# Gates and branch products with the tokens stationary and 512 weight columns streaming

## The reference, cut to what matters

```python
for l in range(2):
    h = _rmsnorm(x, g_mix[l])                       # x: 256 tokens x 1024
    proj = h @ w_in[l]                              # 1024 x 6656
    gate_pre, a_in, na_qkv, dil_qkv, swa_q, swa_kv = split(proj)   # gate_pre: 256 x 4096
    y_a = conformer_conv(a_in)                      # 31 taps, layer norm, silu
    y_b, y_c, y_d = three attentions of 4 heads     # each 256 tokens x 256
    branch[n] = y_n @ w_branch[l][n]                # four products 256x256 @ 256x1024
    gates = sigmoid(gate_pre.reshape(256, 4, 1024) + gate_b[l])
    mixed = sum_n(gates[n] * branch[n])
    x = x + mixed @ w_out[l]
    ...                                             # then the feed-forward part
```

## Time and profile before

| | us |
|---|---|
| median of 3 runs (1650.99 to 1652.85) | 1652.69 |
| the profiled execution's own time | 1651.02 |
| its span, first to last instruction | 1649.3 |
| PE busy | 1604.1 (97%) |
| DVE busy | 1119.4 (68%) |
| ACT busy | 891.5 (54%) |
| POOL busy | 421.6 (26%) |

### The profile page before, as it was taken

How to read it: one execution, slowest core, us unless ns; L and a number is a source line. 1 busy time by engine, 2 the same in 40 slices (tenths; PEclk the granted TensorE clock), 3 DMA queues, 4 the chain that set the end, 5 groups by cost and what they waited for, 6 DMA issues and landing times. The chain is left out here.

```text
span 1649.3 us, 26655 instructions
## 1 busy us (share of the span) xinstructions
PE 1604.1 (97%) x10765; PEld 1440.8 (87%) x10765; DVE 1119.4 (68%) x1587; ACT 891.5 (54%) x1410; POOL 421.6 (26%) x457
## 2 busy tenths in 40 slices
PE   8999999999999999999999999999999999999999
PEld 7868899987877889998888888999888888999997
DVE  6876665645576665655578978777646897867763
ACT  7565544434365455443456756666445684656652
POOL 3401100002341120000146902244204691214430
PEclk9999999999999999999999999999999999999999
DMA  9423366566330236665555345666446444466652
GB/s 352 154 77 129 102 204 185 178 202 206 108 127 27 77 103 179 186 189 188 177 193 166 129 153 161 182 185 191 179 153 219 164 135 149 141 202 190 186 179 76
DMA packets 287386, 267.38 MB, mean 162 GB/s; under 512 B 12320, under 2 KB 247584, under 8 KB 287008
## 3 DMA queue, kind: packets, MB, share of 16 engines
q1 hardware_dynamic: 287264, 265.69, 50.2%
HBM read 264.61 MB, written 1.05 MB: 161 GB/s over the span
## 5 line engine op out<-in xcount | busy, mean ns | idle before, releaser
L146 DVE TENSOR_TENSOR w_lo<-w_raw,w_hi 128x2048 fp32r<-128x2048 f32 x243 | 566.7, 2334 | 263.6 <-ACT w_hi L145 258.7
L145 ACT ACTIVATE w_hi<-w_raw 128x2048 fp32r<-128x2048 f32 x243 | 460.9, 1901 | 227.1 <-PE bank L538 125.5
L1999 PE MATMUL bank<-h_hi,w_hi 128*128 128x256 f32 x1984 | 565.6, 285 | 5.9 <-DVE mix_gates L2838 2.2
L2000 PE MATMUL bank<-h_lo,w_hi 128*128 128x256 f32 x1984 | 561.2, 283 | 0.0
L2001 PE MATMUL bank<-h_hi,w_lo 128*128 128x256 f32 x1984 | 561.1, 283 | 0.0
L1999 PEld LDWEIGHTS bank<-h_hi,w_hi 128*128 128x128 f32 x1984 | 380.3, 192 | 13.6 <-issue 13.1
L2000 PEld LDWEIGHTS bank<-h_lo,w_hi 128*128 128x128 f32 x1984 | 380.5, 192 | 0.1
L2001 PEld LDWEIGHTS bank<-h_hi,w_lo 128*128 128x128 f32 x1984 | 380.5, 192 | 0.0
L465 PE MATMUL bank<-w_hi,h_hi 128*128 128x512 f32 (+1 forms) x288 | 113.0, 392 | 3.8 <-DVE w_lo L242 2.1
L2645 POOL TENSOR_TENSOR mix_conv<-mix_conv,mix_gates 128x512 f32<-128x512 f32 x60 | 109.2, 1821 | 23.8 <-ACT mix_gates L2682 15.8
L3058 POOL TENSOR_TENSOR cffn_hidden<-cffn_conv 128x256 f32<-128x256 f32 x44 | 73.6, 1674 | 155.7 <-ACT cffn_conv L3089 155.7
(11 more groups left out here) (442 smaller groups left out, 2804.6 us busy)
## 6 DMA issues: line engine op xcount, KB each, us to landing
w_raw<-in_w_in SPq DMA_DIRECT2D x48, 1024.0 KB, 4.9
w_raw<-in_ffn_w_in SPq DMA_DIRECT2D x88, 512.0 KB, 4.7
w_raw<-in_w_up SPq DMA_DIRECT2D x88, 512.0 KB, 4.8
w_raw<-in_ffn_w_out SPq DMA_DIRECT2D x22, 1024.0 KB, 4.9
w_raw<-in_w_down SPq DMA_DIRECT2D x22, 1024.0 KB, 4.9
w_raw<-in_nsa_w_in SPq DMA_DIRECT2D x10, 1024.0 KB, 5.3
w_raw<-in_mem_w_kv SPq DMA_DIRECT2D x8, 1024.0 KB, 5.0
w_raw<-in_w_branch SPq DMA_DIRECT2D x8, 1024.0 KB, 4.7
```

Of the source, the lines that this page charges most:

```text
L145: return act.activation(hi, raw, ACT.Copy)
L146: return dve.tensor_tensor(self.lo[:, cut_slot, 0:k * n], raw, hi.bitcast(F32), ALU.subtract)
L1999: pe.matmul(out, h, hi[:, f, :], start=(f == 0), stop=False)
L2000: pe.matmul(out, h, lo[:, f, :], start=False, stop=False)
```

## The change

- **Gates.** A gate job is now a chunk of 4 x 128 rows by 512 gate columns. The tokens are stationary, in two groups of 128 (t), and the 512 columns stream: 2 x 4 x 3 = 24 matmuls, with two jobs for one set q of 512 columns. The result has tokens on the partitions. DVE takes the two banks of a set in a pair, behind the odd job: times the token's factor plus a bias row, `scalar_tensor_tensor`. Bias rows are loaded by 8 more DMAs, spread over the partitions, in three batches with waits on SP. Gate banks turn over 0, 2, 3.
- **Attention.** Values use bank 1 only, transposed pairs bank 6 only; layer norm has bank 7. The waits are one item closer, and DVE splits the values ahead of its copy.
- **Branch products.** Four groups of (half of the features, token group), four branches each, into four banks: tokens stationary, 512 weight columns streaming. DVE multiplies each by its gates, POOL adds the four (3 additions of 128 x 512 a group), PE transposes the sum back (4 transposes a group), ACT rounds it, DVE subtracts. ACT opens the gates of a group in one instruction of 128 x 2048.
- **Output projection.** It waits for the subtraction of group 2 ahead of its first row, makes the last group's transposes ahead of its third row, and waits for that group's subtraction ahead of its fifth.

```diff
     def value(self, m):
-        return self.k.bank[m % 2][:, 0:S]
+        return self.k.bank[1][:, 0:S]
...
-        if m >= 2:
-            pe.wait_ge(self.y_lo, m - 1)
+        if m:
+            pe.wait_ge(self.y_lo, m)
...
-                if j >= 2:
-                    pe.wait_ge(self.copied, j - 1)
+                if j:
+                    pe.wait_ge(self.copied, j)
...
             between(dve, i)
+            if i >= 5 and i % 2:
+                self.dve_values(dve, (i - 5) // 2)
             if 1 <= i <= n:
                 self.dve_copy(dve, i - 1)
-            if i >= 5 and i % 2:
-                self.dve_values(dve, (i - 5) // 2)
...
-        AHEAD, LN_STEP, OPEN = 2, 9, 2
-        gate_banks = [0, 1] + [2, 3] * 4 + [2] + [3] * 5
+        AHEAD, LN_STEP, LN_BANK = 2, 9, 7
+        GROUPS = [(half, t) for half in range(2) for t in range(T)]
+        BRANCHES = [(1, 2, 3, 0)] + [(0, 1, 2, 3)] * 3
+
+        def gate_bank(q, t):
+            return k.bank[(0, 2, 3)[(2 * q + t) % 3]]
...
+                def second_bias(sp):
+                    sp.wait_ge(turn.turned, 6)
+                    load_bias(sp, range(1, 5), gate_bias_in[1])
+
+                def third_bias(sp):
+                    sp.wait_ge(att.masked, 8)
+                    load_bias(sp, range(5, 8), gate_bias_in[2])
...
+                for n in range(len(GROUPS)):
+                    mixed = branch_product(n, 0)
+                    for place in range(1, 4):
+                        pool.wait_ge(mixed_m, 4 * n + place + 1)
+                        if place > 1:
+                            pool.wait_ge(mixed_p, 3 * n + place - 1)
+                        pool.tensor_tensor(mixed, mixed, branch_product(n, place), ALU.add).then_inc(mixed_p, 1)
...
-                    if j < len(gate_chunks):
-                        if j == 12:
+                    if j % 2 and j < len(gate_chunks):
+                        q = j // 2
...
+                        for t in range(T):
+                            dve.scalar_tensor_tensor(out=gates[:, t, q, :], in0=gate_bank(q, t)[:, :],
+                                                     scalar=rows.rstd[:, t:t + 1], in1=gate_bias[q], op0=ALU.mult,
+                                                     op1=ALU.add).then_inc(gated, 1)
...
+                for n in range(len(GROUPS)):
+                    for place in range(4):
+                        multiply(dve, n, place)
+                        if place == 1:
+                            if n >= 2:
+                                mixed_rest(dve, n - 2)
+                        if place == 2 and n < 3:
+                            w.cut_to(dve, (mix_chunks[2], mix_chunks[3], residual.first)[n])
+                mixed_rest(dve, 2)
+                w.cut_to(dve, residual.first + 1)
+                mixed_rest(dve, 3)
...
+                    for t in range(T):
...
+                        if part_of == 0 and 2 * q + t >= 3:
+                            pe.wait_ge(gated, 2 * q + t - 2)
+                        for row in range(4):
+                            f = 4 * part_of + row
+                            x_hi, x_lo = h_hi[:, f, t * P:(t + 1) * P], h_lo[:, f, t * P:(t + 1) * P]
+                            out = gate_bank(q, t)[:, :]
+                            pe.matmul(out, x_hi, whi[:, row, :], start=(f == 0), stop=False)
+                            pe.matmul(out, x_hi, wlo[:, row, :], start=False, stop=False)
+                            ins = pe.matmul(out, x_lo, whi[:, row, :], start=False, stop=(f == KD - 1))
...
+                def mixed_ready_for(pe, f):
+                    if f == 0:
+                        pe.wait_ge(mixed_lo, 3)
+                    if f == 2:
+                        mixed_turn(pe, 3)
+                    if f == 4:
+                        pe.wait_ge(mixed_lo, 4)
```

More of the change, by code:

```diff
@@ L943, in dve_copy @@
         dve.tensor_copy(free(self.k.turned[:, :, :], [[2 * S, 2], [S, T], [1, P]], j % 2 * P),
[L944 removed]
+                        free(self.k.bank[6][:, :], [[S, 2], [P, T], [1, P]])).then_inc(self.copied, 1)
     def dve_values(self, dve, m):
@@ L2697, in _, with open_gates, mixed_round @@
                 project.act(act, squares, hurry=3)
[L2699 to L2702, removed]
+                def open_gates(act, n):
+                    half, t = GROUPS[n]
+                    group = gates[:, t, 4 * half:4 * half + 4, :]
+                    act.activation(group, group, ACT.Sigmoid).then_inc(opened, 1)
+                def mixed_round(act, n):
+                    half, t = GROUPS[n]
+                    act.wait_ge(mixed_turned, n + 1)
+                    act.activation(h_hi[:, 4 * half:4 * half + 4, t * P:(t + 1) * P],
+                                   product_bank(n, 3)[:, :].rearrange("p (f q) -> p f q", q=P), ACT.Copy)\
+                       .then_inc(mixed_hi, 1)
                 w.round_to(act, gate_chunks[2])
@@ L2884, in _ @@
                    .then_inc(ln_lo, 1)
-                att.dve_values(dve, 5)
                 gate(dve, 15)
[L2888 to L2896, removed]
-                    else:
[L2898 to L2908, removed]
-                        dve.wait_ge(mixed_m, 2 * j + 2)
-                        dve.tensor_tensor(part[:, 1, 0:512], k.bank[3][:, :], part[:, 1, 0:512], ALU.add).then_inc(mixed_d, 1)
-                        dve.wait_ge(mixed_d, j)
-                        dve.tensor_tensor(part[:, 1, 0:S], part[:, 1, 0:S], part[:, 1, S:2 * S], ALU.add).then_inc(mixed_d, 1)
-                    if j >= 3 and j % 2 == 1:
-                        w.cut_to(dve, mix_chunks[0] + j // 2 + 2)
-                    if j:
-                        mixed_rest(j - 1)
@@ new lines, in _ @@
+                for n, (half, t) in enumerate(GROUPS):
+                    chunks = mix_chunks[2 * half:2 * half + 2]
+                    if n >= 2:
+                        pe.wait_ge(mixed_m, 4 * (n - 2) + 4)
+                    for place, branch in enumerate(BRANCHES[n]):
+                        if n == 0 and place == 0:
+                            pe.wait_ge(att.y_lo, 6)
+                        if n == 0 and place == 3:
+                            pe.wait_ge(ln_lo, 2)
+                        if n == 1 and place == 0:
+                            pe.wait_ge(gated, 16)
+                        if n >= 2 and place == 3:
+                            pe.wait_ge(mixed_lo, n - 1)
+                        if t == 0:
+                            w.wait_cut(pe, chunks[branch // 2])
+                        whi, wlo = w.halves(chunks[branch // 2])
+                        out = product_bank(n, place)[:, :]
+                        for row in range(2):
+                            f, r = 2 * branch + row, (2 * branch + row) % 4
+                            y, l = y_hi[:, f, t * P:(t + 1) * P], y_lo[:, f, t * P:(t + 1) * P]
+                            pe.matmul(out, y, whi[:, r, :], start=(row == 0), stop=False)
+                            pe.matmul(out, y, wlo[:, r, :], start=False, stop=False)
+                            ins = pe.matmul(out, l, whi[:, r, :], start=False, stop=(row == 1))
+                        if t == 1 and branch % 2 == 1:
+                            ins.then_inc(w.used, 1)
+                        else:
+                            ins.then_inc(mixed_ready, 1)
+                        if n and place == 2:
+                            mixed_turn(pe, n - 1)
```

150 lines of the change are left out of this document (80 added, 70 removed).

## The result

| | before | after |
|---|---|---|
| median of 4 runs, taken in turn (us) | 1652.77 | 1670.26 |
| lowest to highest | 1650.99 to 1654.34 | 1669.58 to 1671.16 |
| profiled execution (span) | 1651.02 (1649.3) | 1671.16 (1669.4) |

The changed kernel takes 1.0107 times as long, 95% interval 1.0089 to 1.0124. Another set of runs of it gave 1670.66 and the same 1.0107 (1.009 to 1.0124). I had forecast 1663.0, at most 1669: the direction is right, the time lies above the range. In what follows a layer is timed from its own first gate job, which starts at 868.76 and 1286.69 before, at 872.20 and 1298.10 after.

What follows compares the result with a forecast made beforehand. PE, busy 97%, was taken as the bound, with DVE setting the pace up to step 5. Per layer +4.85 to the branch products and +1.1 after made +5.95, +11.9 on 1651.02, so 1663; range 1649 to 1669.

Steps and rivals of the forecast that it cites:

- Pitch of the wide form: Gate matmuls of 512 columns start every 0.2267 us, so each of 16 gate jobs saves 0.32.
- Gates on DVE: 16 scalar-times-plus-bias operations at 0.68 us each replace 16 multiplications, now in pairs in even steps.
- wait before gate job 12: PE's 1.11 us wait for the bank that layer norm used goes, as layer norm has bank 7.
- The mid-job wait: In steps 2 and 4 PE waits inside a gate job for DVE's pair, using up its lead; no extra cost.
- V(1): PE's values in step 5 wait about 3 us for DVE's value subtraction and start 5.4 later (3.8 to 6.2).
- the lag of the masks: DVE's masks of step 5, begun at 926.30 before, come 1.6 us later (0 to 2.4).
- From V(1) to the branch products: PE sets the pace: nine gate jobs -2.9, layer norm's bank wait -1.1, value waits in odd steps +3.45.
- Branch products: Wide matmuls -1.3, added transposes +1.7, old waits -1.2, late end 1.9: sum +1.1 us a layer (-0.5 to +2.5).
- The wait at the first row: The output projection waits for DVE's subtraction of group 2, taken as 1.9 us (1.6, or 2.3 if slowed).
- rival 1: Value waits fall into gaps or DVE's lag shrinks, PE's work remains: -7.0 a layer, 1637 or 1642 us; chance 0.13.
- 2 (it cancels): DVE catches up sooner and half of the odd waits is hidden: +0 to +1.5 a layer, 1651 to 1655; chance 0.10.
- Rival 3: GpSimd's additions bound the mixing, at 2.0 us each with DVE's splits at 3.1: +3 a layer, 1669; chance 0.12.

Runs made afterwards that it cites:

- experiment 3: The changed kernel with the gates turning over four banks up to set 3, bank 7 added: 1670.92 us, ratio 1.011.
- experiment 10: The changed kernel with unread matmuls filling PE's waits ahead of the values in steps 5, 7, 9, 11 and in gate job 4: 1665.86 us, ratio 1.0077.
- experiment 5: The changed kernel with group 2's sum turned into bank 0, so the output projection needn't wait for that group's subtraction: 1667.52 us, ratio 1.009.
- experiment 2: The kernel before with all values in bank 1, the wait one item closer and DVE's split ahead of its copy: 1680.56 us, ratio 1.0169.
- experiment 8: The changed kernel once more, unaltered: 1670.66 us.
- experiment 7: The changed kernel with values split a step earlier, group 2's sum turned into bank 0, four gate banks up to set 3: 1649.25 us, ratio 0.9979.
- experiment 1: The changed kernel with the values of m=1 in bank 7, so two value waits reach two steps back again: 1659.2 us, ratio 1.0035.
- experiment 4: The changed kernel with unread matmuls in two waits, 9 in gate job 4 and 14 ahead of V(1): 1668.14 us, ratio 1.0093.
- experiment 9: The kernel before with all values in one bank and their split a step earlier, at the end of the even step: 1652.74 us, ratio 0.9998.

## Why the prediction was wrong

- **Pitch of the wide form**: right, 0.227. A job between attention pieces takes 5.66 instead of 5.91 to 5.95, so 0.25 to 0.29 and not 0.32 each.
- **Gates on DVE**: right in the price, 1.41 a pair, and there is no wait before gate job 12. The mid-job wait was foreseen, as PE's lead being used up, and experiment 3 shows that it is.
- **V(1)**: right in place and cause, and near in size, in part by luck. Less the 3.44 by which layer 0 began later, the masks stand at 927.65 (said 927.9), V(1) at 928.9 (said 929.1): +5.1, in layer 1 +5.8, for +5.4. I said 3 us of wait; it is 3.25. But the lag of the masks has other parts than I said. In layer 0 nothing of it had come up by the masks of step 4 (51.15 us behind the first gate job, 51.23 before), where I had +0.9. All of the 1.35 comes in step 4: 0.7 from the pair, as said, 0.7 from the division (1.73 instead of 1.02) and 0.4 from the weight split (3.35 instead of 2.93), both of which I had left as they were, less idle time of 0.35.
- **From V(1) to the branch products** is the step that failed: the sum had -2.9 - 1.1 + 3.45 = -0.55, measured +1.4 in both layers. In layer 0 the odd steps with a value wait are 3.75 longer for 3.45, steps 10 and 12 are 1.6 shorter for 1.1, and the nine jobs, but for the clock, 2.35 shorter for 2.9: together 0.35 off. The term that isn't in the sum is PE's clock: gate job 7 took 7.12 for 5.66, V(1) 1.13 for 1.02, 1.6 together. I priced a wait at its length. I noted the clock at the higher level in every slice and didn't ask what idle stretches of 3 us, which the kernel before doesn't have in these layers, would do to it.
- **The clock in the kernel before.** I took the page's slices of 41 us at their word. The kernel before has stretches at the lower level itself, outside the mixing layers. From 417.2 to 420.6 it follows an idle time of 1.42 and falls among matmuls of 75 columns. From 461.5 to 468.4 PE had been making matmuls of 32 columns since 459.49, and behind them wide ones start every 0.427 us. Windows of 2 us show it; columns as above:

```profile
462.00:464.00 2.00, 2.00 (x11) 0.50 0.75 242
...
466.00:468.00 2.00, 2.00 (x6) 0.50 0.00 0
```

- **Branch products**: +1.1 up to the output projection, +1.45 up to its last transposes, for +1.1 said. The wait at the first row is 1.47 for 1.9; the products start every 0.227 us as said, but the 96 take 22.45 instead of 21.8, because 0.3 are waited for GpSimd's first sum and the first starts behind each turn are further apart.
- **Start of the sum.** I added to the profiled 1651.0, though the median is 1652.7. This alone put the forecast 1.7 us low, as the prediction states.

Together: the sum gave 1663. Of what it missed, 1.7 come from where it started and 4.4 to 4.8 from the clock (experiment 10 against the changed kernel); and the filled kernel is 13.1 above the kernel before, where the sum had 11.9, so 1.2 are from the other terms. The range's top, 1669, and the sum of all high ends, 1673, took in longer waits but nothing behind them.

**The rivals.** 1 (streaming wins) and 2 (it cancels) fell with the order of DVE: the masks of step 5 come 1.35 later and not at 926. With the order mended the change gives 1651.7 and, with 3 and 5, 1649.2, not the 1637 of rival 1, since up to V(1) PE runs at DVE's pace and what its gates save there is spent waiting: up to V(1) the last one takes 56.3 for 55.0, from V(1) to the branch products 65.5 for 68.1, and 1.6 of the 65.5 are the clock.

Rival 3 (GpSimd the bound of the mixing) came close. The additions, lines of POOL from 1001 to 1023, changed kernel, and its first group in the timeline:

```profile
L2687 POOL TENSOR_TENSOR mix_feat<-mix_feat 128x512 f32<-128x512 f32 x6 | 13.4, 2235 | 28.9 <-DVE mix_feat L2941 28.4
L2687 POOL TENSOR_TENSOR mix_feat<-mix_feat,mix_centred 128x512 f32<-128x512 f32 x2 | 2.6, 1295 | 0.3
```

```profile
1006.98 3.19 POOL L2687 TENSOR_TENSOR mix_feat<-mix_feat 128x512 f32<-128x512 f32 x1
```

The first row is three additions of 1.30 and three of about 3.18, one of these in each group. The one shown begins at 1006.98, 0.25 behind DVE's split (1006.73 to 1009.01), and ends 1.16 behind that. From sum to sum GpSimd takes 6.0 us, almost without a gap, and PE takes 6.0 too. So the rival's price for GpSimd was right (6.0 said); DVE's splits in the groups stayed at 2.3 to 2.8, below the 3.1 it supposed. PE's turns start 0.06 us behind the end of each sum (1011.67, 1017.68 and 1023.66); only ahead of the first does its row of products break off for it, by 0.3. So GpSimd is level with PE here. The Trainium skill's exclusive lock (SBUF — State Buffer, section Who interferes with whom) fits this row: the later one would have waited out the rest of the other, 2.0 of its 3.19 us, and the 1.16 left are near the 1.30 of an addition alone.

## What to carry to other kernels

When a buffer becomes single, the wait is set by where the reader's last access stands in its engine's order, not by the access: moving one instruction of 0.41 us, with the rounding that it needs, a step forward was worth 19 us here. Price an idle stretch of 2 us or more on TensorE at its length and at the stretch of lower clock that may follow it (here 1.6 us, up to 2.9); look for such stretches in windows of 1 or 2 us, also in the kernel before, since the page's slices average them away. And a saving on an engine counts only from the point on where that engine sets the pace.

## What the runs showed of the hardware

**The clock behind waits.** With a wait of 3.2 us or more at V(1), half clock came in every profile and layer (the changed kernel, experiments 2, 3, 5 and 8). In layer 0 of the changed kernel it lasted 3.4 us and cost 1.6. In layer 1 of experiment 5 it lasted 6.8 us, from 1355.1, inside the wait, to 1361.9, with V(1) at 1.91 and gate job 7 at 7.67, and cost 2.9. Behind the wait of 2.69 of experiment 7 it came in both layers. Behind 2.1 us it came in some cases and not in others: at V(4) in experiments 1 and 4 (both layers) and 8 (one), not in the changed kernel and experiments 3 and 5; in gate job 4 in layer 0 of the changed kernel and not in its layer 1. Behind the waits of 0.72, 1.03 and 1.85 of the changed kernel it didn't come. That the waits bring it in these layers is shown by experiment 10, where they are filled and it is gone; what decides in the cases of 2.1 us stays open.

**The start of the run.** The first projection's matmuls start every 0.227 us from 8.93 on in the kernel before. In the changed kernel's profile, with the same code:

```profile
10.08 0.63 PE L467 MATMUL bank<-w_hi,h_lo 128*128 128x512 f32 x1
10.50 0.63 PE L465 MATMUL bank<-w_hi,h_hi 128*128 128x512 f32 x1
...
15.35 0.39 PE L465 MATMUL bank<-w_hi,h_hi 128*128 128x512 f32 x1
```

The starts are 0.427 us apart until about 15, as at half clock, and yet the granted clock's column shows 1.00 there; only the starts tell. The work behind this projection (L1539) begins at 40.89 instead of 37.95. It is no property of a kernel: experiment 9, which is the kernel before up to there, has it (13 such starts), experiments 1 and 7, of the changed form, don't. Over the profiles layer 0's first gate job begins between 868.6 and 872.4, and late where the start was slow. That is about the spread of 3.5 us between runs of one kernel; a sum that starts from one profiled execution inherits it. What sets the state at the start stays open.
